# Decoder layer: expert rows taken out of group B's chains, and the query projection run on the unnormed residual

## The chip, the cores and the metric

The kernel runs on one core of one Trainium2 chip. The metric is the device time of one execution in microseconds (us). Before the change it is 4662.38 us, the median of three runs (4650.35 to 4666.11). The engines are TensorE (PE, with its weight load PEld), VectorE (DVE), ScalarE (ACT), GpSimd (POOL) and SyncE (SP); SP issues most transfers, POOL the indirect gathers.

## The reference, cut to what matters

One layer of a hybrid decoder, for 512 prompt tokens and 8 sample tokens, width 2048. A mixing block of three branches (gated linear attention, a spatial gating unit, cross-attention) is merged and multiplied by `w_out`. What follows is the part that the change is about:

```python
x  = x + merged @ w_out
h  = rmsnorm(x, norm_ffn_g)            # x * rsqrt(mean(x*x) + eps) * g
q  = (h @ w_q)                         # 2048 x 2048: 8 heads, 2 halves of 128
s1 = q[:, :, 0] . sub_k1;  s2 = q[:, :, 1] . sub_k2      # 128 keys each
# per head: the 16 best of each half, then the 16 best of their 256 sums:
# 8 x 16 = 128 experts of each token, with softmaxed gates
a    = peer_u[idx] . h                 # 128 gathered rows of 2048 per token
x    = x + sum(gate * gelu(a) * peer_v[idx])             # 128 more rows
y    = rmsnorm(x, norm_final_g)
```

The norm's divisor is one number per token, so that `(x * g) @ w_q * rstd` equals `h @ w_q`.

## The kernel before, in words

The tokens form two groups. Group A is 264 tokens (two units of 128, and the 8 samples), group B the other 256. Activations lie with their features on the partitions, in 16 tiles of 128. Each weight block is 128 x 2048 values of four bytes (1.05 MB) and gives one tile of 128 outputs. A gathered "row" below is an indirect transfer of one table row for each of 128 tokens: 1.05 MB too.

**Group A** runs first, in split precision: ACT writes a block's high part (`split_hi`, L559), DVE its low part (`split_lo`, L563), and TensorE takes three products per tile (L579). `split` has two slots, so block n + 1 is split while block n is multiplied. A's tail is `sp_out`, `act_out`, `dve_out` and `pe_out` (L2642 to L2801):

- 16 blocks of `w_out`. DVE adds each output to the residual x1, squares it and adds it to `ssum`.
- The norm: a column sum on PE (`pe_spread`), root on ACT, reciprocal on DVE, then 16 tiles h2 = x1 * g * rstd, split in pieces of four tiles. PE turns x1's three units meanwhile (L2758), and ACT copies them out to be stored.
- 16 blocks of `w_q` on h2; ACT copies each output to `pq`. DVE scales B's input `hxb2` once in between.
- After the last block: the key scores of unit 0 (L2765), h2 of unit 0 turned into `htok`, then h2 and the scores of the two other units, each through one of two `stage` buffers and out to DRAM. PE waits for the last of these copies (`staged`), then begins group B.
- DVE finds the experts of head 0 (`top_head`, L2896), and POOL's first gather follows.

**Group B** is multiplied in plain four-byte products (L640) from three `raw` buffers. Its stages are the projections (`dve_project_b`), the merge of branch A (N_BA), attention, the merge of branch C (N_BC), the spatial unit, the merge of branch B (N_BB), and `dve_out_b` with `w_out`, norm and `w_q`.

**A's experts** run beside group B. `experts_a` (L3114) is a generator on DVE: each step is one gathered row, 528 in all: 128 of `peer_u` (`dot`, L3107) and 128 of `peer_v` (`accumulate`, L3112) for each of units 0 and 1, then 16 for the samples. `beside(k)` in B's stages does k of these steps in DVE's program order; the number is written by hand at each place. Heads of later units are found between rows (`head_beside`, one each 14 rows of `peer_v` of unit 0). POOL gathers up to six rows ahead (`ring`), and only after A's last block, since `ring` lies over `split`. 295 rows are done in B's stages.

**The table** (`dve_table`, L3246) is 128 blocks of `peer_u`, multiplied with B's h2 (L3273). DVE's rows are spread evenly over its 128 places, up to row 509 (`U_ROWS`), together with B's 16 heads. ACT does the exponentials and gelus for both at fixed places: `act_gelu` at blocks 30 and 68, `act_soft` at 10, 44, 76 and 108 (L3221 to L3244). DVE's `soft_second` waits for them. Then `dve_last` and `pe_last` do B's experts, 256 more rows.

## Time and profile before

| what | us |
|---|---|
| median of three runs | 4662.38 (4650.35 to 4666.11) |
| the profiled execution | 4664.21 |
| its span in the profile | 4662.5 |
| PE, DVE, ACT, POOL busy | 4116.3, 3098.0, 916.1, 1309.7 |
| DMA over the span | 328 GB/s on average, 1528.97 MB |
| chain that ended last | PE 57%, DMA 22%, DVE 9% |

The span is the program's time between its first and last instruction; the execution's time is 1.7 us longer. In the tables by window, "DMA" is the share of time in which the core's 16 DMA engines were busy, "PEclk" the clock that TensorE was granted (1.00 is 2.4 GHz, 0.50 is 1.2 GHz), and "(x..)" counts instructions.

### The profile page before, as it was taken

What the parts mean: (1) busy time and instruction counts of PE and PEld (TensorE: products, weight loads), DVE (VectorE), ACT (ScalarE), POOL (GpSimd) and SP (SyncE); (2) the same over time, 40 slices, a digit from 0 to 9 for tenths busy, and PEclk for the clock granted to TensorE, in tenths of its full rate; (3) what the DMA queues carried; (4) which work ended last, traced back from release to release, by engine and by line L of the source; (5) the groups of instructions that cost most, each with busy time, mean ns of one, the idle gap of its engine ahead of it and who ended that gap; (6) DMA issues with size and microseconds to landing.
All of it is one profiled execution on the core that took longest, in us unless ns stands there. A gap on an engine that the chain in (4) does not pass through costs nothing.

```text
span 4662.5 us, 61529 instructions
## 1 busy us (share of the span) xinstructions
PE 4116.3 (88%) x23624; PEld 3587.9 (77%) x23624; DVE 3098.0 (66%) x4546; ACT 916.1 (20%) x1325; POOL 1309.7 (28%) x822
## 2 busy tenths in 40 slices
PE   7999999999899999999886788999999999577555
PEld 7999999999789887887775677887888888353222
DVE  7434344435557557887678786797788357688776
ACT  4334433324333321110000000000000004000100
POOL 0000000000000013444345233343345231467665
PEclk9999999999899999999998798999999999787777
DMA  5555678766356469999999799999899897999998
GB/s 215 197 205 190 220 282 294 274 242 206 124 206 234 164 265 410 414 393 404 423 388 404 314 405 408 393 423 414 354 414 423 357 364 277 412 406 399 422 421 356
DMA packets 303262, 1528.97 MB, mean 328 GB/s; under 512 B 36394, under 2 KB 108538, under 8 KB 134948
## 3 DMA queue, kind: packets, MB, share of 16 engines
q0 software_dynamic: 114288, 830.54, 43.3%
q1 hardware_dynamic: 188772, 695.78, 39.6%
q8 instruction: 122, 2.00, 0.2%
q14 instruction: 80, 0.66, 0.0%
HBM read 1450.06 MB, written 76.13 MB: 327 GB/s over the span
## 4 chain that ended last, share of the span: by engine, by line
PE 57%; DMA 22%; DVE 9%; issue 5%; DVEq 3%; POOL 3%; ACT 2%; ACTq 0%; SPq 0%; POOLq 0%
PE psum L579 27%; PE psum L3273 14%; DMA sb_ring<-in_peer_v,sb_idx_all 8%; PE psum L640 7%; DMA sb_raw<-in_wstream 4%; DMA sb_ring<-in_peer_u,sb_idx_all 3%; DMA sb_raw_u<-in_wstream 3%; POOL sb_ring L3086 2%; PE psum L3529 2%; DVE sb_ring L3107 1%; DVE sb_acc L3112 1%; PE psum L2325 1%; DVE sb_acc_b L3430 1%; PE psum L3511 1%; DVEq L2354 1%
## 5 line engine op out<-in xcount | busy, mean ns | idle before, releaser
L579 PE MATMUL psum<-sb_actr,sb_split 128*128 128x264 f32 x8112 | 1010.6, 286 | 36.5 <-DVE sb_split L563 20.4
L579 PEld LDWEIGHTS psum<-sb_actr,sb_split 128*128 128x128 f32 x8112 | 999.2, 190 | 42.4 <-issue 25.9
L563 DVE TENSOR_TENSOR sb_split<-sb_raw,sb_split 128x2048 fp32r<-128x2048 f32 x201 | 460.5, 2292 | 638.2 <-ACT sb_split L559 637.1
L2997 POOL DMA_INDIRECT sb_ring<-in_peer_u,sb_idx_all x256 | 413.2, 1614 | 1172.1 <-DVE sb_dots L3107 550.3
L3112 DVE SCALAR_TENSOR_TENSOR sb_acc<-sb_ring,sb_coef,sb_acc 128x2048 f32<-128x2048 f32 x256 | 601.7, 2350 | 130.7 <-DMA sb_ring<-in_peer_v,sb_idx_all 115.5
L3107 DVE CUSTOM_DVE_ANT_0 sb_ring<-sb_ring,sb_htok 128x2048 f32<-128x2048 f32 x264 | 594.8, 2290 | 128.7 <-DMA sb_ring<-in_peer_u,sb_idx_all 123.1
L2997 POOL DMA_INDIRECT sb_ring<-in_peer_v,sb_idx_all x256 | 433.3, 1693 | 667.8 <-DVE sb_acc L3112 575.3
L3529 PE MATMUL psum<-sb_ring,sb_diag 128*128 128x512 f32 x512 | 343.5, 833 | 244.4 <-DMA sb_ring<-in_peer_v,sb_idx_all 237.3
L3430 DVE SCALAR_TENSOR_TENSOR sb_acc_b<-sb_ring,sb_coef_b,sb_acc_b 128x2048 f32<-128x2048 f32 x192 | 451.3, 2351 | 133.2 <-DMA sb_ring<-in_peer_v,sb_idx_all 119.5
L3086 POOL DMA_INDIRECT sb_ring<-in_peer_v,sb_idx_all x256 | 431.3, 1685 | 270.7 <-DVE sb_acc_b L3430 130.3
L3529 PEld LDWEIGHTS psum<-sb_ring,sb_diag 128*128 128x128 f32 x512 | 132.3, 272 | 440.2 <-DMA sb_ring<-in_peer_v,sb_idx_all 270.6
L3273 PE MATMUL psum<-sb_h2b,sb_raw_u 128*128 128x256 f32 x2048 | 453.0, 381 | 12.0 <-DMA sb_raw_u<-in_wstream 10.1
L3273 PE MATMUL psum<-sb_h2b,sb_raw 128*128 128x256 f32 x2048 | 451.3, 380 | 9.8 <-DMA sb_raw<-in_wstream 9.7
L3273 PEld LDWEIGHTS psum<-sb_h2b,sb_raw_u 128*128 128x128 f32 x2048 | 388.5, 191 | 72.9 <-DMA sb_raw_u<-in_wstream 18.4
L3273 PEld LDWEIGHTS psum<-sb_h2b,sb_raw 128*128 128x128 f32 x2048 | 387.3, 190 | 70.1 <-DMA sb_raw<-in_wstream 18.2
L559 ACT ACTIVATE sb_split<-sb_raw 128x2048 fp32r<-128x2048 f32 x201 | 384.4, 1913 | 203.1 <-PE psum L579 168.1
L640 PE MATMUL psum<-sb_hxb,sb_raw 128*128 128x256 f32 x1824 | 406.3, 385 | 8.3 <-DMA sb_raw<-in_wstream 6.3
L640 PEld LDWEIGHTS psum<-sb_hxb,sb_raw 128*128 128x128 f32 x1824 | 350.3, 193 | 60.7 <-DMA sb_raw<-in_wstream 8.6
L579 PE MATMUL psum<-sb_actb_hi,sb_split 128*128 128x256 f32 x1664 | 299.8, 279 | 0.0
L579 PEld LDWEIGHTS psum<-sb_actb_hi,sb_split 128*128 128x128 f32 x1664 | 257.0, 188 | 0.0
L579 PE MATMUL psum<-sb_actb_lo,sb_split 128*128 128x256 f32 x832 | 232.2, 279 | 0.0
L3229 ACT ACTIVATE sb_a_tile<-psum 128x128 f32<-128x128 f32 x128 | 35.5, 278 | 852.2 <-PE psum L3273 852.2
(446 smaller groups left out, 4216.7 us busy)
## 6 DMA issues: line engine op xcount, KB each, us to landing
sb_raw<-in_wstream SPq DMA_DIRECT2D x398, 1024.0 KB, 7.8
sb_raw_u<-in_wstream SPq DMA_DIRECT2D x64, 1024.0 KB, 16.3
sb_states<-in_state SPq DMA_DIRECT2D x32, 512.0 KB, 3.9
sb_states_t<-in_stateT SPq DMA_DIRECT2D x32, 512.0 KB, 4.4
out_gla_s<-sb_states SPq DMA_DIRECT2D x32, 512.0 KB, 3.1
dram_z<-sb_zst SPq DMA_DIRECT2D x121, 132.0 KB
dram_z_b<-sb_zst SPq DMA_DIRECT2D x65, 128.0 KB
sb_vrow<-dram_v SPq DMA_DIRECT2D x8, 1024.0 KB, 5.4
```

What stands on the lines that cost most here:

```text
L559: nc.scalar.activation(split[:, slot, 0, :], raw[:, slot, :], ACT.Copy).then_inc(hi_ready, 1)
L563: nc.vector.tensor_tensor(split[:, slot, 1, :], raw[:, slot, :], split[:, slot, 0, :], ALU.subtract).then_inc(lo_ready, 1)
L579: last = nc.tensor.matmul(psum[:, bank, 0:ntok], w[a], acts(b, kt), start=(i == 0 and a == 0 and b == 0), stop=(i == len(kts) - 1 and a == 1))
L640: last = nc.tensor.matmul(bank_b(q), raw[:, k % 3, w0 + i * P:w0 + (i + 1) * P], acts[:, kt, 0:WB], start=(i == 0), stop=(i == len(kts) - 1))
L2325: last = nc.tensor.matmul(psum[:, 6 + j % 2, 0:WB], raw[:, k % 3, kt * P:(kt + 1) * P], hxb2[:, kt, :], start=(kt == 0), stop=(kt == KT - 1))
L2997: nc.gpsimd.indirect_dma_start(ring[g % RING][:], None, ins[table], bass.IndirectOffsetOnAxis(ap=col, axis=0)) \
L3086: nc.gpsimd.indirect_dma_start(ring_b[slot_b(y, n)][:], None, ins["peer_v"], bass.IndirectOffsetOnAxis(ap=idx_all[:, 3 + y, n:n + 1], axis ...
L3107: nc.vector.tensor_tensor_reduce(u[:], u[:], htok[:], 1.0, 0.0, ALU.mult, ALU.add, out).then_inc(row_used, 1)
L3112: nc.vector.scalar_tensor_tensor(out=a[:], in0=v[:], scalar=c, in1=a[:], op0=ALU.mult, op1=ALU.add).then_inc(row_used, 1)
L3273: last = nc.tensor.matmul(bank_b(OUTS_U + i), raw_u[u_slot(i)][:, kt * P:(kt + 1) * P], h2b[:, kt, :], start=(kt == 0), stop=(kt == KT - 1))
L3430: nc.vector.scalar_tensor_tensor(out=acc_b[y][:], in0=v[:], scalar=coef_b[y][:, n:n + 1], in1=acc_b[y][:], op0=ALU.mult, op1=ALU.add).then ...
L3529: last = nc.tensor.matmul(psum[:, b, :], diag[:, n // PE_EACH % DIAGS, :], v[:, b * 512:(b + 1) * 512], start=(n < PE_EACH), stop=(n >= SL ...
```

## The change

In A's tail the products of `w_q` start on x1 * g, tile by tile as `w_out`'s outputs come, without waiting for the norm; `rstd` is multiplied in where DVE now evicts `pq`. Blocks are split two ahead. The turnings of x1 and h2, and the scores of the first four heads, are put between the `w_q` blocks on PE. Two heads of unit 0 are routed on DVE, in halves, during blocks 11 to 14; later ones are found two heads ahead of their rows. `h2` now lies in x1's place, and `stage0` alone takes x1's three units.

In B's stages 33 `beside` steps go away: 6 in the first merge, 6 in attention, 8 in the merge of branch C, 8 in the spatial unit, 5 in the norm. The total is fixed, so these rows are done in the table.

```diff
+        h2 = x1
+        gx1_hi = sb("gx1_hi", [P, KT, WA], F32R, R_M + 16896)
+        gx1_lo = [sb("gx1_lo0", [P, 7, WA], F32R, R_RAW + 16384), ...
@@ load_b: B's third raw buffer
+                if k == 2:
+                    sp.wait_ge(out_ready, OUTS_A)
@@ dve_attention
-                    beside(2)
                     maxima(h + 2)
-                    beside(1)
                     divide(h + 2)
@@ dve_spatial
                 norm_gv_first(dve, g, u)
-                beside(3)
                 norm_gv_second(dve, g, u)
                 if u > 0:
-                    beside(1)
                     gate_gv(dve, g, u - 1)
-            beside(1)
             gate_gv(dve, g, g.units - 1)
@@ stage_of
-            return k % 2 if k < STAGED_A else (k - STAGED_A) % 2
+            return 0 if k < 3 else k % 2 if k < STAGED_A else (k - STAGED_A) % 2
@@ act_out
+            for j in range(KT):
+                split_next(act, N_OUT + j)
+                act.wait_ge(evac_done, out_of(N_OUT + j) + 1)
+                nc.scalar.activation(gx1(0, j), x1[:, j, :], ACT.Copy, scale=pcols[:, C_FFN + j:C_FFN + j + 1])
+                if j > 0:
+                    act.wait_ge(act_lo, 20 + j)
+                nc.scalar.activation(sq2[:], x1[:, j, :], ACT.Square).then_inc(act_hi, 1)
@@ dve_out
+            for j in range(KT):
+                n = N_OUT + j
+                dve.wait_ge(out_ready, out_of(n) + 1)
+                nc.vector.tensor_tensor(x1[:, j, :], pair_of(n % 2), x1[:, j, :], ALU.add).then_inc(evac_done, 1)
+                split_lo(dve, n + 2, n % 2)
+                dve.wait_ge(act_hi, 20 + j + 1)
+                nc.vector.tensor_tensor(ssum[:], ssum[:], sq2[:], ALU.add)
+                nc.vector.scalar_tensor_tensor(out=gx1(1, j), in0=x1[:, j, :], scalar=pcols[:, C_FFN + j:C_FFN + j + 1],
+                                               in1=gx1(0, j), op0=ALU.mult, op1=ALU.subtract).then_inc(act_lo, 1)
+            for c in range(16):
...
+                nc.vector.tensor_tensor(pq[:, c, :], pair_of(n % 2), rstd[:], ALU.mult).then_inc(evac_done, 1)
+                if n + 2 < N_END:
+                    split_lo(dve, n + 2, n % 2)
+                if 2 <= c < 6:            # hxb2, four tiles in each
...
+                if c in (6, 7):           # h2, eight tiles in each
...
+                if HEAD_AT <= c < HEAD_AT + 2 * HEADS_AHEAD:
+                    half_head_ahead(dve, *divmod(c - HEAD_AT, 2))
@@ pe_out: after block c of w_q; X1_AT, H2_AT, SCORE_AT, HEAD_AT = (2, 4, 6), 8, 10, 11
+                if c == H2_AT:
+                    pe.wait_ge(staged, 3)
+                    pe.wait_ge(normed, 10)
+                    turn_unit(h2, 0, 4).then_inc(turned, 1)
+                if c == SCORE_AT:
+                    pe.wait_ge(htok_ready, 1)
+                    score_unit(0, 4, range(8)).then_inc(scored, 1)
+            pe.wait_ge(evac_done, OUTS_A)
+            score_unit(0, 4, range(8, KT)).then_inc(scored, 1)
@@ dve_out_b
-            beside(6)
+            beside(1)
@@ experts_a
-            top_head(dve, 0, 0)
-            dve.drain().then_inc(idx_ready, 1)
...
+                    if t == 0 and n % TOP == 0 and n // TOP + HEADS_AHEAD < PH:
@@ vector's program
-            dve_merge_b(dve, N_BA, N_BC, beside, lambda k: 3 if k < GATES_B else 2)
+            dve_merge_b(dve, N_BA, N_BC, beside, lambda k: 3 if k < GATES_B and k % 2 == 0 else 2)
-            dve_merge_b(dve, N_BC, N_BB, beside, lambda k: 2 - k % 2)
+            dve_merge_b(dve, N_BC, N_BB, beside, lambda k: 1)
```

## Rows read from the trace of the kernel before

**Rows 1.** Windows: start:end, length, busy of each engine, PEclk, DMA share, GB/s.

```profile
1683.00:1703.00 20.00, 17.34 (x147) 15.46 (x148) 12.01 (x57) 11.10 (x7) 3.01 (x3) 1.00 0.39 148
1703.00:2222.00 519.00, 487.44 (x2367) 418.82 (x2365) 409.73 (x591) 69.99 (x137) 208.44 (x130) 0.97 0.99 405
2222.00:2426.00 204.00, 183.79 (x832) 160.56 (x832) 142.93 (x178) 11.65 (x20) 83.42 (x49) 0.95 0.99 410
2426.00:2462.00 36.00, 23.85 (x81) 18.74 (x82) 29.45 (x49) 8.67 (x25) 19.45 (x10) 0.74 0.94 361
2462.00:2551.00 89.00, 59.82 (x256) 50.41 (x255) 76.38 (x104) 1.03 (x1) 44.80 (x22) 0.86 1.01 410
2551.00:2596.00 45.00, 19.81 (x56) 12.38 (x56) 39.48 (x65) 2.09 (x4) 13.78 (x10) 0.50 0.74 277
2596.00:2669.00 73.00, 60.40 (x256) 51.44 (x256) 56.80 (x84) 0.43 (x1) 18.08 (x15) 0.92 0.84 336
2669.00:2823.00 154.00, 121.48 (x546) 105.78 (x546) 123.76 (x155) 4.17 (x3) 54.95 (x42) 0.87 1.00 409
```

**Rows 2.** Windows of the table, the whole and three parts; columns as in group 1.

```profile
2952.00:3870.00 918.00, 897.46 (x4098) 776.03 (x4098) 679.53 (x1161) 65.57 (x270) 370.07 (x222) 1.00 0.96 392
3242.00:3300.00 58.00, 57.20 (x264) 49.73 (x263) 15.93 (x42) 5.16 (x18) 9.32 (x6) 1.00 0.73 281
3300.00:3682.00 382.00, 373.75 (x1710) 322.97 (x1710) 322.50 (x518) 27.53 (x114) 177.68 (x98) 1.00 1.01 418
3682.00:3760.00 78.00, 77.50 (x358) 67.60 (x357) 19.60 (x11) 5.10 (x23) 14.90 (x9) 1.00 0.69 261
```

**Rows 3.** Timeline of PE in A's tail: start, us, what, [idle before <-releaser].

```profile
1569.00 0.71 PE L1238 MATMUL psum<-sb_ssum,sb_ones 128*128 128x264 f32 x2 [1.71 <-DVEq L2730]
1570.23 7.13 PE L2758 MATMUL psum<-sb_ident,sb_x 128*128 128x128 f32 x48 [0.53 <-DVE sb_ssum L2732]
...
1683.26 3.81 PE L2765 MATMUL psum<-sb_keys,sb_pq 128*128 128x128 f32 x32 [0.61 <-ACTq L2698]
...
1702.36 27.89 PE L640 MATMUL psum<-sb_hxb,sb_raw 128*128 128x256 f32 x128 [1.96 <-ACT sb_stage L2635]
```

**Rows 4.** Groups by line, 1605 to 1683: count, busy us, mean ns.

```profile
L579 PE MATMUL psum<-sb_actr,sb_split 128*128 128x264 f32 x624 | 77.1, 287 | 2.9 <-DVE sb_split L563 2.9
...
L563 DVE TENSOR_TENSOR sb_split<-sb_raw,sb_split 128x2048 fp32r<-128x2048 f32 x13 | 29.7, 2292 | 43.2 <-ACT sb_split L559 42.9 <-issue 0.3
L559 ACT ACTIVATE sb_split<-sb_raw 128x2048 fp32r<-128x2048 f32 x12 | 22.9, 1910 | 0.1
```

**Rows 5.** Timeline of DVE: one head, its first operation, its middle, its last.

```profile
1689.09 0.49 DVE L2904 MAX8 sb_top_v<-sb_sc 128x8 f32<-128x128 f32 x2 [13.38 <-ACT sb_sc L2700]
...
1692.45 0.18 DVE L2920 CAST sb_top_if<-sb_top_i 128x32 f32<-128x32 uint32 x1
...
1698.15 0.18 DVE L2946 SCALAR_TENSOR_TENSOR sb_idx_all<-sb_e_f 128x16 uint32<-128x16 f32 x1
```

**Rows 6.** Chain of waits, 1690 to 1740: a small store once gathers run.

```profile
1709.98 13.36 DMA dram_z_b<-sb_zst
```

**Rows 7.** Groups of DVE by line, 1703 to 2952: expert rows.

```profile
L3112 DVE SCALAR_TENSOR_TENSOR sb_acc<-sb_ring,sb_coef,sb_acc 128x2048 f32<-128x2048 f32 x128 | 300.7, 2349 | 44.6 <-DMA sb_ring<-in_peer_v,sb_idx_all 38.1 <-DVE sb_acc L3112 1.4 <-issue 0.3
```

**Rows 8.** Timeline of PE in B's stages: where it waited for DVE.

```profile
2426.36 6.14 PE L2063 MATMUL psum<-sb_kvt,sb_xq 128*128 128x256 f32 x16 [9.37 <-DVE sb_merged L2352]
...
2551.47 3.68 PE L2409 MATMUL psum<-sb_ident,sb_gv_b 128*128 128x128 f32 x16 [13.21 <-DVE sb_zst L2352]
...
2586.00 2.07 PE L2420 MATMUL psum<-sb_bspat,sb_ones 1*128 1x512 f32 x2 [12.58 <-DVE sb_vn L2518]
...
2823.49 84.98 PE L640 MATMUL psum<-sb_h2b,sb_raw 128*128 128x256 f32 x384 [15.55 <-DVEq L2859]
```

**Rows 9.** Timeline of DVE in the table: its two long waits for ACT.

```profile
3283.77 0.29 DVE L2965 TENSOR_REDUCE sb_sums<-sb_gate_all 128x8 f32<-128x128 f32 x1 [41.15 <-ACT sb_gate_all L2975]
...
3738.95 0.29 DVE L2965 TENSOR_REDUCE sb_sums<-sb_gate_all 128x8 f32<-128x128 f32 x1 [63.11 <-ACT sb_gate_all L2975]
```

More of the change, by code:

```diff
@@ L593, in of_b, with gx1 @@
             return actb[b][:, kt, :]
+        def gx1(b, kt):
+            return gx1_lo[kt // 7][:, kt % 7, :] if b else gx1_hi[:, kt, :]
         def of_br2(b, kt):
@@ L2560, in dve_spatial_beside, with dve_spatial @@
                 gated_lo(dve, 2)
-        def dve_spatial(dve, g, beside):
+        def dve_spatial(dve, g):
             dve.wait_ge(vn_stored, 16)
@@ L2650, in sp_out @@
             wide_loop(sp, N_OUT + 4, N_WQ, lambda n, slot, u, m, j: load_block(sp, n + 3, 1 - slot))
-            for u in range(3):
-                store_stage(sp, u, x1_dram[x1_rows(GA, u), :], unit(u)[0])
-            wide_loop(sp, N_WQ, N_END - 4, lambda n, slot, u, m, j: load_block(sp, n + 3, 1 - slot))
-            load_block(sp, N_END - 1, (N_END - 1) % 2)
+            for n in range(N_WQ, N_END - 3):
+                load_block(sp, n + 3, (n + 3) % 2)
+                if n - N_WQ in (4, 6, 8):
+                    u = (n - N_WQ - 4) // 2
+                    store_stage(sp, u, x1_dram[x1_rows(GA, u), :], unit(u)[0])
             for k in range(3):
@@ L2665, in act_out @@
             act_piece(act, merged, 3)
-            wide_loop(act, N_OUT, N_WQ, lambda n, slot, u, m, j: split_hi(act, n + 1, 1 - slot, u + 1 + slot, m))
-            act.wait_ge(sums_ready, 6)
-            act.wait_ge(root_in, ROOTS_X1[0] + 1)
-            nc.scalar.activation(rstd[:], ssum[:], ACT.Sqrt).then_inc(root_out, 1)
-            def x1_stage(u):
-                rows = unit(u)[0]
-                act.wait_ge(turned, u + 1)
-                fill_stage(act, u, rows, psum[0:rows, 4 - 4 * (u % 2):8 - 4 * (u % 2), :])
@@ new lines, in act_out @@
+            for j in range(KT):
[6 more added lines that the diff above has]
+            for c in range(16):
+                split_next(act, N_WQ + c)
+                if c == 0:
+                    act.wait_ge(root_in, ROOTS_X1[0] + 1)
+                    nc.scalar.activation(rstd[:], ssum[:], ACT.Sqrt).then_inc(root_out, 1)
+                if c in X1_AT:
+                    u = X1_AT.index(c)
+                    rows = unit(u)[0]
+                    act.wait_ge(turned, u + 1)
+                    fill_stage(act, u, rows, psum[0:rows, 4:8, :])
+                if c == H2_AT:
+                    act.wait_ge(turned, 4)
+                    nc.scalar.activation(htok[:].rearrange("p (b f) -> p b f", b=4), psum[:, 4:8, :], ACT.Copy).then_inc(htok_ready, 1)
+                if c == SCORE_AT:
+                    act_scores(act, 0)
@@ L2709, in act_out, with act_scores @@
                 rows = unit(1 + k)[0]
-                act.wait_ge(scored, 2 + k)
+                act.wait_ge(scored, 3 + k)
                 fill_stage(act, 5 + k, rows, psum[0:rows, 4 * (k % 2):4 * (k % 2) + 4, :])
+        def act_scores(act, half):
+            act.wait_ge(scored, half + 1)
+            nc.scalar.activation(sc[0][:, 4 * half:4 * half + 4].rearrange("p h a k -> p (h a k)").rearrange("p (b f) -> p b f", b=2),
+                                 psum[:, 4 + 2 * half:6 + 2 * half, :], ACT.Copy).then_inc(sc_ready_b, 1)
         def dve_out(dve):
@@ L2733, in dve_out @@
-            dve.wait_ge(root_out, ROOTS_X1[0] + 1)
-            nc.vector.reciprocal(rstd[:], rstd[:])
-            dve.drain()
-            for q in range(4):
-                for kt in range(4 * q, 4 * q + 4):
-                    nc.vector.scalar_tensor_tensor(out=h2[:, kt, :], in0=x1[:, kt, :], scalar=pcols[:, C_FFN + kt:C_FFN + kt + 1],
-                                                   in1=rstd[:], op0=ALU.mult, op1=ALU.mult)
-                dve.drain().then_inc(normed, 1)
-                if q > 0:
-                    dve_piece(dve, h2, 20, q - 1)
@@ L2759, in turn_unit, with score_unit @@
             return last
-        def score_unit(u, b0):
+        def score_unit(u, b0, tiles=range(KT)):
             rows, tok = unit(u)
-            for c in range(KT):
+            for c in tiles:
                 last = nc.tensor.matmul(psum[0:rows, b0 + c // 4, (c % 4) * P:(c % 4 + 1) * P],
@@ L2773, in body @@
                 pe.wait_ge(evac_done, m - 1)
-                products(pe, slot, of_a, range(KT), 0, 2 * slot, WA, ready=ready).then_inc(out_ready, 1)
+                products(pe, slot, acts, range(KT), 0, 2 * slot, WA, ready=ready).then_inc(out_ready, 1)
             body(N_OUT, N_OUT % 2, None, N_OUT + 16, 0, ready=lambda kt: wait_piece(pe, kt, 16))
@@ L2948, in top_head, with half_head_ahead @@
             dve.drain()
+        def half_head_ahead(dve, k, half):
+            if half == 0:
+                dve.wait_ge(pool_made, 1)
+                dve.wait_ge(sc_ready_b, 1)
+                top_first(dve, 0, k)
+            else:
+                top_second(dve, 0, k)
+                dve.drain().then_inc(idx_ready, 1)
         def heads_of(x, t):
@@ L3644, in _ @@
             dve_out_b(dve, beside)
-            assert 270 < gone[0] < 300, gone
+            assert 250 < gone[0] < 300, gone
             dve_table(dve, beside, gone[0])
```

175 lines of the change are left out of this document (84 added, 91 removed).

## The prediction

> **What bounds the kernel now.** I read the windows first, stage by stage, because the engines' shares of the whole span hide that the limit changes. From the first gather on it is the DMA engines: they are busy 0.99 to 1.01 of B's projections, first merge, merge of branch C and output stage, and of most of the table [rows 1, 2], at 405 to 418 GB/s. What follows the table is not edited, and I let it stand. So the reader should count two things: bytes, which the change leaves alone, and time in which the DMA engines idle. That idle time, (1 - share) times length, is 12 us in 1683 to 1703, 5 + 2 + 2 in the next three windows, 12 in the spatial unit, 12 in the merge of branch B [rows 1], and 16 + 24 in the table's two holes [rows 2] (by its whole share of 0.96 it would be 37): 85 us in all.
>
> The second view is PE's timeline. In B's stages it stands still for DVE, not for data: 9.37 us before attention, 13.21 before the spatial unit, 12.58 inside it, 15.55 before `w_q` [rows 8]. DVE was late because rows stood ahead of B's work in its program: one is 2.35 us [rows 7], one head 9.2 us (1689.09 to 1698.33) [rows 5]. The third view is DVE's timeline in the table, where it is the other way round: DVE waits 41.15 and 63.11 us for ACT's exponentials, which stand at fixed blocks [rows 9]. Rows have room there, in B's chains they have none.
>
> **Price of a moved row.** 1.05 MB at the 418 GB/s of 3300 to 3682 [rows 2] is 2.5 us of DMA, more than its 2.35 us of DVE. 33 rows are 83 us of DMA wherever they go.
>
> **Part 1, A's tail.** One `w_q` block is 48 products, 77.1 / 624 x 48 = 5.9 us [rows 4]. PE's last `w_out` product ends at 1569.00 - 1.71 = 1567.3, its last `w_q` product at 1683.26 - 0.61 = 1682.6 [rows 3]. These 115.3 us hold 16 x 5.9 = 94.4 us of blocks, and 0.7 and 5.7 of column sum and x1's turnings (7.13 less waits): 14.5 us idle, round the norm. The change lets `w_q` begin at once, so this goes. Added to this stretch: h2's turning (16 where x1 has 48, so 1.9) and half of unit 0's scores, 3.81 / 2 = 1.9 [rows 3]. New waits, from DVE's order. Per block DVE needs 1.91 (ACT's high part) + 2.29 + 0.45 for the eviction [rows 4]: 4.7 of 5.9 us. (a) `rstd` between blocks 0 and 1: about 1 us late. (b) h2 is scaled in 16 operations over blocks 6 and 7 and PE waits for the last: 2 us. (c) A head's second half is 5.9 us (1692.45 to 1698.33), its first 3.4 [rows 5]. The second halves at blocks 12 and 14 do not fit into 5.9 - 4.7: the first delays block 15 by 1.8 us, the second delays the last eviction, and with it the scores, by 4.4. Extra copies on ACT (0.4 us each) fit beside its 1.9 of 5.9 us. So the last block ends 14.5 - 3.8 - 1 - 2 - 1.8 = 5.9 us earlier, near 1677, and gathers may start then instead of behind head 0, at 1698.33 or later.
>
> But what follows is not earlier by as much. B's first product waits for the last staged copy (the 1.96 us) [rows 3], and that copy waits in `stage1` for the store of h2's unit 1. Before, that store went out ahead of the gathers. Now it goes out some 10 us after six gathers of 1.05 MB were issued. The nearest row is the small store that took 13.36 us once gathers ran [rows 6]; the other bound is one transfer's own 2.5 us. I take 13: the second scores wait 4.4 us for the eviction and take 1.9, a turning 1.9, a copy 1.9 (10 in all), the store 13, two copies 1.9 each: 1677 + 27 = 1704, a little less where they overlap, against 1702.36. B's start: **0** (bounds -7 and +5).
>
> The Trainium skill, page "DMA: Bandwidth & Descriptors", section "Queues, rings and completion order", says that each DMA engine takes turns between its queues, packet by packet. Beside one gather queue the store would then have half of the rate, 5 us instead of 13, and B would begin near 1695; the row of 13.36 us speaks against counting on it.
>
> **Part 2, B's projections.** The 131 rows stay. DVE has two heads (18 us) behind it, and six rows are in the ring 20 us earlier. Of PE's 32 us of waits there (519 - 487) [rows 1] part is for DVE. But the share is 0.99: what can be won is the earlier 15 us of DMA work, and PE must use it. I take **-8** (0 to -18).
>
> **Part 3, the chains.** First merge: 6 rows are 14 us of DVE, which clears the 9.37 us wait [rows 8]; of the 11 us in which PE waits for weights, 4 more: **-13** (-6 to -20). Attention, 36 us with PE busy 24 at a clock of 0.74: DVE's answers no longer sit behind one or two rows: **-7** (-4 to -9). Merge of branch C: 89 us at share 1.01, PE busy 60 at clock 0.86; 8 rows are 20 us of DMA, and a head (9.2) goes with them; the 13.21 us DVE wait vanishes and most weight waits: **-25** (-14 to -32), down to about PE's 60. Spatial: 8 rows and one head, 8 x 2.35 + 9.2 = 28 us of DVE, PE 20 us at the low clock 0.50; the waits of 10 and 12.58 go, its own chain of norms stays: **-18** (-12 to -22). Merge of branch B: **-2**. Output stage: five rows in front of the norm are -13, but the heads shift with the row count and one more falls into its 32 rows, +6 of its 9.2: **-7** (0 to -13). Sum of part 3: **-72**. The clock needs no term of its own: it is in the durations of those windows.
>
> **Part 4, the table.** It gets 247 rows instead of 214. Before it took 918 us (2952 to 3870) with 40 of DMA idle: 878 busy. Plus 83 is 961; with DVE's two long waits gone the idle time falls to near nothing. PE is busy for 897 [rows 2], so the DMA decides: 960, **+42**. Lower bound +15: the rows fill the two holes and the rest is paid by DMA time that weight loads do not need at the end. Upper +60, if rows starve the weight loads as well. ACT's block 30 needs the 64th dot of unit 1, row 320, which stands at place 30 of DVE's program (it was 15): at 1.93 x 2.35 + 9.2/4 = 6.8 us of DVE per place against 7.2 of PE it is just in time.
>
> **Sum.** 0 - 8 - 72 + 42 = **-38** against the profiled 4664.2: 4626. The median of the runs is 1.8 us lower, so 4662.4 - 38 = **4624 us**. The check: 85 us of idle DMA, less 38 gained, plus 6 from the earlier end of A, leaves 53 us idle, which the now row-free spatial and attention stages (some 15 and 10), projections and ends can hold.
>
> **Rivals.**
> (1) *The DMA keeps its sum.* Every stage but two had a share near 1; taking rows out of B's chains makes DMA idle there exactly as much as it fills up in the table. For it: the spatial unit already idles with rows beside it (0.74) and the ring holds only six. Against: the waits of rows 8 are on DVE, and the chain of waits goes through them. Then only the earlier gathers count: -8 to -12, 4652. The Trainium skill, page "Perfetto Trace Analysis", section "Identifying the Most-Contended Engine", says that interleaving regimes with different limits may help; this change undoes such an interleaving.
> (2) *Slower: the table pays full price and starves.* With both waits gone DMA is saturated through all 128 blocks, each weight load stands behind six gathers, and ACT stands at block 30 until DVE reaches row 320. It decides if DVE needs over 7.2 us per place in the first 30. The table then takes +83 and 15 for stalls, B's chains give -60 and B's start +5, projections -8: +35, about 4697.
> (3) *The table absorbs nearly all.* +10 there, with parts 2 and 3 at their better ends (-15, -72): 4585.
> (4) The rows move, but A's tail, where DVE now evicts, splits, scales and routes, is late by more than computed. It costs at most 10 us and moves no sign; it is in the range. That the change does not do what it says I see no way for: the counts are in program order.
>
> **How the numbers follow.** Forecast 0.58, (1) 0.16, (2) 0.08, (3) 0.18. Spreads of the terms added by size give 4624 +- 22; reaching to (3) and to (1) the range is **4585 to 4657**. A measurement of this kernel can tell some 0.3% (14 us) from nothing: faster means below 4648. From the forecast 0.55, from (3) 0.18, from (1) 0.04: **faster 0.77**; same 0.03 + 0.12 = **0.15**; slower **0.08**.
>
> **What would show it.** Part 1: `w_q`'s first product within 1 us of `w_out`'s last; gaps of some 2 us before block 15 and 4 before the second scores; a first gather near 1678; B's first product near 1702, waiting for a staged copy that waits for a store. Part 3: the four waits of rows 8 below 3 us, B's stages to the table 80 us shorter, with a DMA share under 0.6 in the spatial unit. Part 4: the table near 960 us, share above 0.98, DVE's waits for ACT under 10 us. Wrong is the forecast if the table grows by over 60 us or under 15, or if the chains give under 50.

## The result, and the profile after

The changed kernel takes **4640.62 us** (median of 8 runs, 4634.76 to 4648.66), the kernel before, beside it on the same chip, 4663.74 us (8 runs, 4650.35 to 4668.09). The ratio is 0.9948, with a 95% interval of 0.9937 to 0.9960: 0.5% faster, by 23 us where 38 were forecast. The profiled execution took 4642.09 us with a span of 4640.0, against 4662.5 before.

Read the windows first, as for the kernel before. Their columns are those of [rows 1].

```profile
2222.00:2418.00 196.00, 184.27 (x832) 160.91 (x832) 121.05 (x136) 12.71 (x20) 74.22 (x44) 0.97 0.96 391
2418.00:2454.00 36.00, 19.84 (x87) 16.32 (x88) 19.75 (x55) 9.60 (x25) 2.03 (x3) 0.81 0.60 235
2454.00:2530.00 76.00, 58.67 (x260) 50.68 (x259) 55.83 (x84) 0.00 (x0) 14.69 (x15) 0.87 0.97 395
2530.00:2555.00 25.00, 19.40 (x53) 11.93 (x52) 13.03 (x17) 2.52 (x4) 0.07 (x1) 0.57 0.20 79
...
2890.00:3846.00 956.00, 909.42 (x4098) 770.66 (x4098) 754.68 (x1228) 65.23 (x268) 401.75 (x256) 1.00 1.01 417
```

The spatial unit (2530) is 25 us long instead of 45 and leaves the DMA engines idle for 0.80 of it. The table (last line) is 956 instead of 918 us, at a share of 1.01 where it was 0.96: its 40 us of idle DMA are gone.

The timeline of PE, where it waits in A's tail and in B's stages, answers to [rows 3] and [rows 8]:

```profile
1565.25 0.28 PE L582 MATMUL psum<-sb_gx_hi,sb_split 128*128 128x264 f32 x1
...
1629.97 3.65 PE L2778 MATMUL psum<-sb_ident,sb_x 128*128 128x128 f32 x16 [5.52 <-DVEq L2770]
...
1672.53 0.36 PE L582 MATMUL psum<-sb_gx_hi,sb_split 128*128 128x264 f32 x1 [2.10 <-DVE sb_split L566]
...
1682.61 3.78 PE L2785 MATMUL psum<-sb_keys,sb_pq 128*128 128x128 f32 x16 [4.01 <-DVE sb_pq L2753]
...
1705.23 5.00 PE L648 MATMUL psum<-sb_hxb,sb_raw 128*128 128x256 f32 x14 [6.72 <-ACT sb_stage L2642]
...
1864.65 3.07 PE L1782 MATMUL psum<-sb_qi_b,sb_ki_b 128*32 128x32 f32 x32 [13.77 <-DVEq L1939]
...
2418.34 3.72 PE L2071 MATMUL psum<-sb_kvt,sb_xq 128*128 128x256 f32 x16 [0.52 <-DVE sb_merged L2358]
2435.56 1.11 PE L2108 MATMUL psum<-sb_ident,sb_prob 128*128 128x128 f32 x4 [13.49 <-DVE sb_prob L2180]
...
2502.24 16.64 PE L648 MATMUL psum<-sb_brb,sb_raw 128*128 128x256 f32 x64 [8.02 <-DMA sb_raw<-in_wstream]
2528.19 3.48 PE L2415 MATMUL psum<-sb_ident,sb_gv_b 128*128 128x128 f32 x16 [9.31 <-DVE sb_zst L2358]
2534.87 2.04 PE L2426 MATMUL psum<-sb_bspat,sb_ones 1*128 1x512 f32 x2 [3.20 <-DVE sb_vn L2524]
...
2761.25 4.21 PE L648 MATMUL psum<-sb_h2b,sb_raw 128*128 128x256 f32 x9 [2.34 <-DVEq L2887]
```

Of the four waits of [rows 8] (9.37, 13.21, 12.58, 15.55 us) three are at 0.52, 3.20 and 2.34; the one before the spatial unit is still 9.31. New ones stand beside them: 13.49 us inside attention, 13.77 at the first chunk product of the projections (5.08 before), 8.02 for a weight block.

**One correction before stages are compared.** Executions differ ahead of anything that was edited: `w_out`'s last product in A ends at 1567.3 before and at 1565.3 after, and in the twelve experiments between 1557.3 and 1567.6. So all that follows is in lengths, from that product to the table's last block, and not in times of the clock:

| stage, us | before | after | change | forecast |
|---|---|---|---|---|
| A's tail, to B's first product | 135.1 | 140.0 | +4.8 | 0 |
| projections | 529.2 | 530.7 | +1.5 | -8 |
| first merge | 194.8 | 182.4 | -12.4 | -13 |
| attention | 35.4 | 34.2 | -1.2 | -7 |
| merge of branch C | 89.7 | 75.7 | -14.0 | -25 |
| spatial unit | 45.0 | 25.2 | -19.8 | -18 |
| merge of branch B | 72.8 | 72.5 | -0.3 | -2 |
| output stage, to `w_q` | 154.2 | 135.4 | -18.8 | -7 |
| `w_q` of B | 128.7 | 129.0 | +0.3 | |
| table | 917.9 | 956.3 | +38.4 | +42 |
| sum | 2302.8 | 2281.4 | -21.4 | -38 (rounded) |

The sum, the 2.0 us by which this execution was early and 1.0 us more after the table make the 22.5 us between the spans.

Each length is read from one execution, and lengths repeat unequally where the code of a stage is the same. A's tail comes out at 140.0 to 140.3 us in the six kernels that have the changed one and at 135.1 to 136.3 in the three with the old one. The projections take 529.2 to 534.0 us in the three with the old tail and 524.1 to 533.0 in five with the new one. From the table's last product to the end of the program, which nothing edits, it is 788.4 to 798.3 us. So 2 us tell something in the tail, and 5 us in the projections or in a sum can be the execution's own.

What the table pays is seen in two waits views of it, first of the kernel before, then after (columns: engine, line, releaser; us in total, times, the longest):

```profile
DVE sb_sums L2965 <- ACT sb_gate_all L2975: 104.8, 3, 63.1
...
PE psum L3273 <- DMA sb_raw_u<-in_wstream: 10.1, 21, 1.4
PE psum L3273 <- DMA sb_raw<-in_wstream: 9.7, 20, 1.4
```

```profile
PE psum L3318 <- DMA sb_raw_u<-in_wstream: 23.8, 46, 1.4
PE psum L3318 <- DMA sb_raw<-in_wstream: 22.4, 46, 1.4
...
DVE sb_sums L3011 <- ACT sb_gate_all L3021: 16.2, 1, 16.2
```

DVE's long waits for ACT shrank from 104.8 to 16.2 us, and PE's waits for weights grew from 19.8 to 46.2. With PE's busy time up from 897.5 [rows 2] to 909.4 this is the whole of the 38.4 us (26.4 + 12.0). In the chain of waits of the changed kernel the table is now this pattern, over and over, where the chain before had 3% of the span in that transfer and now has 11%:

```profile
3289.46 23.01 DMA sb_raw_u<-in_wstream
...
3312.51 7.19 PE psum L3318 x32
...
3319.72 24.01 DMA sb_raw_u<-in_wstream
```

### The profile page after: what moved, and what is told of

It reads as the page before. It is cut to its first block, busy times and chain, and to the rows that moved or that the text cites. A ratio compares the mean times of both kernels' runs of the same rounds, so it can differ in the third digit from the quotient of the medians.

```text
span 4640.0 us, 61274 instructions
## 1 busy us (share of the span) xinstructions
PE 4125.0 (89%) x23624; PEld 3579.6 (77%) x23624; DVE 3099.4 (67%) x4558; ACT 918.0 (20%) x1338; POOL 1288.8 (28%) x822
## 4 chain that ended last, share of the span: by engine, by line
PE 55%; DMA 26%; DVE 8%; issue 4%; POOL 2%; DVEq 2%; ACT 2%; SPq 0%; ACTq 0%; POOLq 0%
PE psum L582 28%; DMA sb_raw_u<-in_wstream 11%; PE psum L648 9%; PE psum L3318 9%; DMA sb_ring<-in_peer_v,sb_idx_all 7%; DMA sb_ring<-in_peer_u,sb_idx_all 3%; POOL sb_ring L3132 2%; DMA sb_raw<-in_wstream 2%; PE psum L3574 2%; PE psum L2331 1%; DVE sb_acc L3158 1%; DVE sb_ring L3153 1%; PE psum L3556 1%; DVE sb_acc_b L3475 1%; DVE sb_split L566 1%
## 5 line engine op out<-in xcount | busy, mean ns | idle before, releaser
L582 PE MATMUL psum<-sb_actr,sb_split 128*128 128x264 f32 x7344 | 913.3, 286 | 29.5 <-DVE sb_split L566 18.4
L582 PEld LDWEIGHTS psum<-sb_actr,sb_split 128*128 128x128 f32 x7344 | 903.1, 190 | 33.9 <-issue 18.9
L3043 POOL DMA_INDIRECT sb_ring<-in_peer_u,sb_idx_all x256 | 428.8, 1675 | 1118.8 <-PE psum L582 519.8
L3043 POOL DMA_INDIRECT sb_ring<-in_peer_v,sb_idx_all x256 | 392.4, 1533 | 719.0 <-DVE sb_acc L3158 632.0
L3132 POOL DMA_INDIRECT sb_ring<-in_peer_v,sb_idx_all x256 | 435.7, 1702 | 267.7 <-DVE sb_acc_b L3475 144.2
```

Of the source, the lines that this page charges most:

```text
L582: last = nc.tensor.matmul(psum[:, bank, 0:ntok], w[a], acts(b, kt), start=(i == 0 and a == 0 and b == 0), stop=(i == len(kts) - 1 and a == 1))
L3043: nc.gpsimd.indirect_dma_start(ring[g % RING][:], None, ins[table], bass.IndirectOffsetOnAxis(ap=col, axis=0)) \
L3132: nc.gpsimd.indirect_dma_start(ring_b[slot_b(y, n)][:], None, ins["peer_v"], bass.IndirectOffsetOnAxis(ap=idx_all[:, 3 + y, n:n + 1], axis ...
```

## The experiments

Twelve kernels. "Before" stands beside each on the same chip; the median is in us, the ratio is to the kernel before. "Tail", "chains" (B's first product to the table's first), "table" and their "sum" are lengths in the profiled execution; "rows" is how many rows more than before the table does.

| kernel | rows | tail | chains | table | sum | median (runs) | ratio (95%) |
|---|---|---|---|---|---|---|---|
| before | 0 | 135.1 | 1249.8 | 917.9 | 2302.8 | 4663.7 | |
| tail_only | 0 | 140.2 | 1253.2 | 914.4 | 2307.8 | 4663.88 (10) | 1.0010 (1.0000 to 1.0019) |
| spatial_only | 8 | 136.3 | 1226.6 | 915.5 | 2278.4 | 4635.84 (5) | 0.9953 (0.9940 to 0.9967) |
| fifteen | 15 | 134.6 | 1209.3 | 923.5 | 2267.4 | 4626.45 (5) | 0.9921 (0.9908 to 0.9934) |
| rows_back | 19 | 140.1 | 1206.6 | 927.9 | 2274.5 | 4632.82 (6) | 0.9946 (0.9927 to 0.9964) |
| twenty | 20 | 136.3 | 1196.9 | 931.1 | 2264.3 | 4623.36 (6) | 0.9918 (0.9905 to 0.9931) |
| four_edits | 26 | 136.4 | 1182.8 | 945.2 | 2264.4 | 4621.52 (5) | 0.9919 (0.9906 to 0.9933) |
| rows_only | 33 | 136.2 | 1192.0 | 957.5 | 2285.7 | 4644.77 (8) | 0.9960 (0.9949 to 0.9972) |
| after | 33 | 140.0 | 1185.1 | 956.3 | 2281.4 | 4640.62 (8) | 0.9948 (0.9937 to 0.9960) |
| early_rows | 33 | 140.1 | 1175.2 | 956.8 | 2272.0 | 4634.24 (4) | 0.9944 (0.9927 to 0.9961) |
| stores_early | 33 | 135.2 | 1183.8 | 957.1 | 2276.0 | 4636.84 (5) | 0.9947 (0.9929 to 0.9964) |
| att_head | 34 | 140.3 | 1173.5 | 961.6 | 2275.3 | 4638.02 (5) | 0.9959 (0.9945 to 0.9973) |
| all_three | 34 | 136.2 | 1166.4 | 963.5 | 2266.2 | 4626.44 (6) | 0.9921 (0.9905 to 0.9938) |
| more_out | 41 | 140.1 | 1182.3 | 967.5 | 2289.8 | 4644.66 (8) | 0.9963 (0.9950 to 0.9976) |

### The two halves of the change

**tail_only**: A's tail as changed, all of B's `beside` numbers as before (in attention, the spatial unit and the output stage too).

```diff
-            dve_merge_b(dve, N_BA, N_BC, beside, lambda k: 3 if k < GATES_B and k % 2 == 0 else 2)
+            dve_merge_b(dve, N_BA, N_BC, beside, lambda k: 3 if k < GATES_B else 2)
...
-            dve_merge_b(dve, N_BC, N_BB, beside, lambda k: 1)
+            dve_merge_b(dve, N_BC, N_BB, beside, lambda k: 2 - k % 2)
...
```

> Group A's tail as changed, but B's stages with all the rows they had before (295, none moved to the table). Theory (the rows carry the gain, the tail almost none): A's last block ends 4 us earlier, but B's first product still waits for a staged copy behind a store of h2, so B begins at 1705 +- 3 and its first merge at 2227 +- 5; the table begins at 2950 to 2958; total within 8 us of the kernel before, 4656 to 4672. Rival (the tail and the 20 us earlier gathers carry it): the first merge begins by 2212, total 4650 or less.

**rows_only**: the kernel before, with the 33 rows taken out.

> Group A's tail as before, the 33 rows moved from B's stages to the table. Theory (DVE's lateness in the chains was the price, DMA in the table pays for part of it): first merge begins at 2223 as before, table at 2887 to 2893, table 38 us longer (918 to 956); total -24 to -32 against before, 4632 to 4640. Rival (rows only change places while the DMA engines are the bound): table begins earlier by no more than it grows, total within 8 us of before.

The new tail alone is worth nothing: 1.0010, and its length is 5 us more than before, not less. The rows alone bring 15 us in the median and 17.1 in the sum of lengths, below what was expected of them. So the gain comes from the rows, and the query projection's early start, the larger part of the diff, gives none by itself. Whether it adds a little once the rows are out is not shown: the changed kernel is at 0.9948 and rows_only at 0.9960, with intervals that overlap, and their sums are 4.3 us apart.

### What the tail loses

**stores_early**: SP issues the stores of x1's three units one block earlier (the blocks at which PE turns them and ACT copies them into `stage0` stay).

```diff
-                if n - N_WQ in (4, 6, 8):
-                    u = (n - N_WQ - 4) // 2
+                if n - N_WQ in (3, 5, 7):
+                    u = (n - N_WQ - 3) // 2
```

> The changed kernel with the three stores of x1's units issued one query-projection block earlier each, behind blocks 3, 5 and 7 instead of 4, 6 and 8. Now ACT waits 5.8 and 7.5 us for them, writes block 8's high part late, and PE waits 5.5 us before h2's turning. Theory: that wait falls to 2 us (h2's scaling by DVE alone), A's last block ends 3 to 5 us earlier, near 1674; B's first product follows it by 26 us as before, near 1701; B's projections still end at 2232 +- 5, since DVE and the rows set that, so the total is within 4 us of the changed kernel's 4641. Rival (time won in A's tail is won in the total): -4 us or more.

The changed kernel's timeline of ACT shows why h2's turning was 5.52 us late, not the 2 that the forecast gave it:

```profile
1605.46 1.88 ACT L2642 ACTIVATE sb_stage<-psum 128x2048 f32<-128x2048 f32 x1 [5.78 <-DMA dram_x<-sb_stage]
...
1620.57 1.87 ACT L2642 ACTIVATE sb_stage<-psum 8x2048 f32<-8x2048 f32 x1 [7.50 <-DMA dram_x<-sb_stage]
```

All three units go through `stage0`, each copy waits for the store of the one before, and ACT's split of the next block stands behind it in its program. With the stores a block earlier the copies of the second and the third unit have no wait, and PE's is 1.92 (timelines of ACT and PE of stores_early):

```profile
1611.82 1.86 ACT L2642 ACTIVATE sb_stage<-psum 8x2048 f32<-8x2048 f32 x1
```

```profile
1625.22 2.91 PE L2778 MATMUL psum<-sb_ident,sb_x 128*128 128x128 f32 x16 [1.92 <-DVEq L2770]
...
1677.67 3.45 PE L2785 MATMUL psum<-sb_keys,sb_pq 128*128 128x128 f32 x16 [4.02 <-DVE sb_pq L2753]
```

The last block now ends 109.6 us after `w_out` (1677.67 - 4.02 - 1564.08), where the forecast's own figures give 1677 - 1567.3 = 109.7; in the changed kernel it is 113.3. The tail is 135.2 us, as before the change. The 5 us are in the trace; the medians can't tell them (0.9947 against 0.9948).

That even this tail wins nothing is the other end of it, which the forecast had: the chain of waits of the changed kernel before B's first product.

```profile
1689.14 1.89 ACT sb_stage L2642
...
1691.05 10.42 DMA dram_h<-sb_stage
...
1703.33 1.86 ACT sb_stage L2642
...
1705.23 29.61 PE psum L648 x128
```

h2's store took 10.42 us among the gathers that had started earlier. By the Trainium skill's rule of turns between queues ("DMA: Bandwidth & Descriptors", "Queues, rings and completion order") the estimate was 5; the trace does not bear out a half share for the store.

### What the projections lose

**early_rows**: the same 131 rows in B's projections, but more of them early.

```diff
-            beside(7)
+            beside(13)
...
-            beside(3)
+            beside(6)
...
-            beside(26)
+            beside(17)
```

> The changed kernel with nine rows of B's projections earlier: 13 instead of 7 before the decay's first step, 6 instead of 3 before its second, 17 instead of 26 in front of the first products; the count at the end of the stage is the same. DVE now idles 45 of 60 us there with the ring full, and PE later waits 13.8 us for it. Theory: that wait falls to under 3 us, the first merge begins 8 to 13 us earlier (2214 to 2219), total 4628 to 4634. Rival (rows are held by their landing, not by where they stand): the wait falls but weight loads come late by as much, first merge within 3 us of 2227, total 4638 to 4643.

Windows at the start of the projections, of the changed kernel and of early_rows:

```profile
1703.00:1723.00 20.00, 17.77 (x74) 15.40 (x75) 2.63 (x4) 3.01 (x5) 4.08 (x3) 0.86 1.01 425
1723.00:1743.00 20.00, 20.00 (x84) 16.71 (x83) 6.75 (x11) 0.89 (x4) 0.24 (x1) 0.91 0.80 300
1743.00:1763.00 20.00, 20.00 (x94) 17.61 (x93) 4.04 (x5) 9.10 (x12) 4.81 (x3) 1.00 0.87 354
1763.00:1783.00 20.00, 20.00 (x95) 17.60 (x94) 19.43 (x25) 1.92 (x9) 5.67 (x3) 1.00 0.68 247
```

```profile
1727.00:1747.00 20.00, 18.94 (x79) 15.78 (x79) 10.20 (x15) 0.89 (x4) 4.62 (x3) 0.91 1.01 412
1747.00:1767.00 20.00, 18.76 (x85) 15.55 (x84) 18.21 (x47) 8.98 (x12) 8.38 (x6) 1.00 1.02 427
1767.00:1787.00 20.00, 12.96 (x47) 10.61 (x46) 19.07 (x25) 1.15 (x5) 6.76 (x4) 0.74 1.01 416
```

In the changed kernel DVE, two heads ahead, has done its first rows by 1706 and then stands before the decay step, with 2.63, 6.75 and 4.04 us of work in 20. The view of its waits from 1700 to 1765, POOL's with them:

```profile
POOL sb_ring L3043 <- DVE sb_dots L3153: 35.1, 1, 35.1
DVE sb_bcum L1999 <- PE psum L1790: 30.3, 1, 30.3
DVE sb_bcum L2007 <- ACT sb_gy L1870: 16.0, 1, 16.0
```

The ring is full, POOL sends no gather for 35.1 us, and the DMA share falls to 0.80, 0.87, 0.68: (0.20 + 0.13 + 0.32) x 20 = 13 us of idle DMA, about what the earlier gathers had won. It is missed later: in the chain of waits ahead of the first chunk product (the wait of 13.77 us) stand a gather of 19.27 us, a head and rows:

```profile
1826.23 19.27 DMA sb_ring<-in_peer_u,sb_idx_all
```

With six more rows early the share is 1.01 and that wait is gone; the projections take 516.7 us instead of 530.7, the first merge gives 4.6 of it back (187.0), and the sum of lengths is 9.4 lower. The two stages together take 703.3 to 706.8 us in the three kernels with these rows early and 711.0 to 716.0 in the five that are otherwise alike in them, so this is more than one execution's luck. The two ratios do not tell it (0.9944 and 0.9948).

### What attention loses

**att_head**: the one `beside(1)` that the change left in attention goes too.

```diff
             maxima(1)
-            beside(1)
             divide(0)
```

> The changed kernel less the one row that is left in B's attention (it goes to the table). That row is the one that carries a head: 9.3 us of head and 2.4 of row stand between the maxima and the division, and PE waits 13.5 us. Theory: the head falls behind attention into the merge of branch C, where PE is four outputs ahead; attention 34 to 24 us, total -6 to -10 against the changed kernel, 4630 to 4635. Rival (the DMA engines are the bound there, so that the time only moves): attention shorter, the merge of branch C or the table longer by as much, total within 3 us.

The changed kernel's timeline of DVE in attention:

```profile
2422.95 0.48 DVE L2934 MAX8 sb_top_v<-sb_sc 128x8 f32<-128x128 f32 x2
...
2432.31 2.35 DVE L3158 SCALAR_TENSOR_TENSOR sb_acc<-sb_ring,sb_coef,sb_acc 128x2048 f32<-128x2048 f32 x1
2434.58 0.16 DVE L2178 RECIPROCAL sb_small<-sb_small 128x2 f32<-128x2 f32 x1
```

That single step is a row at which a head falls due, so it costs 9.2 + 2.35 us between `maxima(1)` and `divide(0)`: the 13.49 us of PE's wait. Without it the wait is 1.86 us and attention 20.8 us:

```profile
2420.29 0.66 PE L2108 MATMUL psum<-sb_ident,sb_prob 128*128 128x128 f32 x4 [1.86 <-DVE sb_prob L2180]
```

Of these 13.4 us the merge of branch C takes 4 back (the head is found there) and the table is 5 longer, with a 34th row in it. In the medians nothing is left of it (0.9959 against 0.9948), so that the -6 to -10 expected for the total are not borne out.

### What a row costs in the table

**rows_back**: of the changed kernel's 33 rows, the 8 of the spatial unit and the 6 of attention go back. **more_out**: 8 more rows leave the merge of branch B. **spatial_only**: the kernel before, with only the spatial unit's 8 out.

```diff
@@ rows_back, in dve_attention and dve_spatial
+                    beside(2)
...
+                    beside(1)
...
+                beside(3)
...
+                    beside(1)
...
+            beside(1)
@@ more_out
-            dve_merge_b(dve, N_BB, N_OUT, beside, lambda k: 1)
+            dve_merge_b(dve, N_BB, N_OUT, beside, lambda k: k % 2)
@@ spatial_only, in dve_spatial
-                beside(3)
...
-                    beside(1)
...
-            beside(1)
```

> The changed kernel with 14 rows put back from the table: 8 in the spatial unit, 6 in attention. Theory (a row in the now saturated table costs a whole 2.5 us of DMA, in the spatial unit 2.35 us of DVE plus a head of 9.3): spatial unit 25 to 45 us, attention 34 to 36 or less if the head falls elsewhere, the table 956 to 921 to 926; total -5 to -12 against the changed kernel, 4629 to 4636. Rival (rows beside a chain are the worst place, as the change has it): total +10 or more, the table shorter by 15 at most, since DVE again waits for ACT's fixed places in it.

> The changed kernel with 8 more rows out of the merge of branch B (one at every second output), so 255 in the table. Theory (the table is saturated, each row costs it 2.5 us; in the merge, PE busy 59 of 72 us, they cost little): table 956 to 976, merge of branch B 72 to 64, total +10 to +14, 4651 to 4655. Rival (the table still has room for rows): total within 3 us or below.

> The kernel before with only the spatial unit's 8 rows taken out (they are done in the table). The forecast put -18 on this part, and the changed kernel shows the stage 20 us shorter. Theory A (the rows only change their place: the DMA pays for them in the table, at the 2.0 us a row that the kernel with 14 rows put back showed, 28.4 us of table for 14 rows): spatial unit 45 to 25, merge of branch B and the rest unchanged, table +8 to +16 longer, total -4 to -10 and perhaps nothing that can be told. Theory B (the spatial unit's idle DMA time is won for good, since the table of before has 40 us of idle DMA of its own to take the rows): table +4 at most, total -15 to -18, about 4645.

Spatial_only is the surprise of the study: **eight rows alone give 24 us, as much as the whole change** (0.9953 against 0.9948). The unit is 20 us shorter, the merge of branch B 7.7 (65.1), and the table does the eight rows in 2.4 us less than before (in 1.1 more than in tail_only, the other kernel with none). Of the theories on record the one that had these rows paid for in the table fell; the other (-15 to -18 us) was right in kind, and too low for a reason that it did not name. The window and the waits of its table:

```profile
2920.00:3836.00 916.00, 896.67 (x4101) 774.92 (x4102) 698.14 (x1177) 65.49 (x270) 387.90 (x230) 1.00 0.98 402
```

```profile
DVE sb_sums L2962 <- ACT sb_gate_all L2972: 78.0, 3, 45.2
...
PE psum L3270 <- DMA sb_raw_u<-in_wstream: 10.7, 22, 1.4
PE psum L3270 <- DMA sb_raw<-in_wstream: 7.9, 21, 0.4
```

The 7.7 us of the merge of branch B do not look like the rows' own. The number of rows done before a stage also sets where in it the next head falls. The merge takes 64.8 and 65.1 us in the two kernels in which its head stands behind the fourth or fifth of its 16 rows (four_edits and spatial_only), and 71.1 to 73.0 in the eleven in which it stands behind the eleventh or twelfth. Timeline of DVE, in spatial_only 21 us into the stage (it begins at 2572.4), in the kernel before 48 us into it (2596.5):

```profile
2593.48 0.48 DVE L2901 MAX8 sb_top_v<-sb_sc 128x8 f32<-128x128 f32 x2
```

```profile
2644.13 0.48 DVE L2904 MAX8 sb_top_v<-sb_sc 128x8 f32<-128x128 f32 x2
```

Waits of DVE in that stage, of spatial_only and of the kernel before:

```profile
DVE sb_zst L2352 <- PE psum L640: 6.2, 5, 5.3
```

```profile
DVE sb_zst L2352 <- DMA sb_gt<-dram_z_b: 4.0, 1, 4.0
DVE sb_zst L2352 <- DMA sb_gt_b<-dram_z_b: 3.2, 2, 2.1
```

With a late head DVE first waits for the loads of the gates, 5.9 to 7.4 us in all eleven, and then finds the head on top of it. With an early one it is behind from then on and waits for them 0.0 and 0.4 us. No run moved the head alone, but the traces leave some 17 of the 24 us to the rows. The spatial unit's own 20 us hold a head too: four_edits has the eight rows there and no head, and takes 36.2 us, so that the rows are worth 11 and the head 9.

The rows went into DVE's waits for ACT and the DMA idle time beside them (share 0.96 to 0.98), and PE's waits for weights stayed at 18.6 us (19.8 before). Read down the table of runs: with 0, 8, 15, 19, 20, 26, 33, 34 and 41 rows the table is 914 to 918, 916, 924, 928, 931, 945, 956 to 958, 962 to 964 and 968 us. The first eight are free, the next eleven or so cost 1 us each, and from 20 rows to 34 it is (962.6 - 931.1) / 14 = 2.2 us each, near the 2.5 us of DMA that a row needs. The last point does not go on like that: from 33 rows to 41 it is 11.2 us, 1.4 each, and from 20 to 41 1.7 on average. So the price rises once the idle time is filled, but over no longer stretch does a row pay the whole 2.5. Rows_back shows the other side: the last 14 rows shortened the chains by 21.5 us (1206.6 - 1185.1) and lengthened the table by 28.4. Some 20 of the 21.5 are the spatial unit's (45.2 there); the 7.9 us that attention gains by its six rows the merge of branch C gives back (67.9 us in rows_back, 75.7 after). These 6.9 us of sum are not told by the ratios (0.9946 against 0.9948). More_out: eight rows out of the merge of branch B bring 12.9 us there (59.6), the output stage gives 7.9 back, the table pays 11, where 20 were expected of it.

### Versions made from it

**all_three** is att_head, early_rows and stores_early together; **four_edits** is that with the spatial unit's 8 rows back; **fifteen** is all_three with the rows of the first merge, of the merge of branch C and of the norm back, so that only attention (7) and the spatial unit (8) are free of rows; **twenty** is fifteen without the norm's five.

> The changed kernel with all three edits: no row in B's attention, nine rows earlier in B's projections, x1's stores one block earlier. Theory: attention's -8 and the projections' -7 lie in different stages and add; the stores add nothing: table to begin near 2868, select near 3832, total 4624 to 4629. Rival (what is won before the table is lost in it): 4632 to 4637, no better than either alone.

> The kernel with three edits (no row in attention, rows later in B's projections, x1's stores one block earlier; 4626.4, 0.9921) and the spatial unit's 8 rows put back. If the rows of the spatial unit are free or better there, as the kernel with 14 rows put back suggested (33 rows moved gave 4640.6, 19 rows moved 4632.8): spatial unit 45 us instead of 25, table about 940 instead of 963, total 4615 to 4625. Rival: the gain of putting rows back belonged to the table's ends or to attention's rows, and with the other three edits the last 8 are worth nothing or cost: 4627 to 4640.

> The kernel with three edits, and of its 34 rows out of B's chains only the 15 of attention (7) and the spatial unit (8) stay out; the first merge, the merge of branch C and the norm of the output stage have theirs back. Theory C (a row's price in the table is marginal: nothing for about the first 16, which fill its idle 40 us of DMA, and 2 to 2.5 us for each after that; read from 8 rows -2 us, 19 rows +10, 33 rows +38, 41 rows +50): table 918 to 926. Attention 21 us, spatial unit 25, merge of branch B 65 to 69; the first merge and the merge of branch C near 190 and 85 to 90; from B's first product to the end of the table 2120 to 2128 (2130 with 34 rows), total 4616 to 4624. Rival D (every row costs 1.2 us there, as 38 us for 33 suggests): table 936, total 4628 to 4636.

> The same with 20 rows out: also the five ahead of the output stage's norm. Theory C: the output stage 10 to 15 us shorter than with 15 rows, the table 928 to 934, so within 6 us of the kernel with 15 rows, 4614 to 4624, since rows past the 16th pay 2 to 2.5 us each. Rival D: table 942, 4622 to 4632. Neither asks for more than 5 us below the kernel with three edits (4626).

All four beat both kernels, by 0.8% against before: 4621.52 to 4626.45 us, with intervals that overlap. The spatial unit's eight rows put back (four_edits) change nothing that can be told, 0.9919 against 0.9921 for all_three. In fifteen and twenty the table came out as the marginal price says (923.5 and 931.1; the rival of 1.2 us a row asked for 936 and 942), but the chains of fifteen were longer than expected, so that B's first product to the end of the table was 2132.8 us and not 2120 to 2128, and the median of 4626.45 lies above the 4616 to 4624 on record. Its merge of branch C holds 22 rows and two heads, 22 x 2.35 + 2 x 9.2 = 70 us of DVE where PE needs 60, and in the kernel before 23 rows and one head; it takes 94.2 us (89.7 before), and the spatial unit waits (timeline of PE in fifteen):

```profile
2529.33 3.04 PE L2414 MATMUL psum<-sb_ident,sb_gv_b 128*128 128x128 f32 x13 [22.80 <-DVE sb_zst L2357]
```

With 15, 20, 26 and 34 rows out, the sum of lengths of these four stays within 2264 to 2268 us. There each row out of a chain wins about what the table asks for it, and how many are out hardly matters any more. Some 7 us of four_edits are those of the early head in the merge of branch B.

## Why the prediction was right or wrong

**Right:** the direction, the range (4585 to 4657) and the main mechanism: PE stood behind rows in DVE's program, and the table took these rows in for less than their full DMA price. Part 3 as a sum: -72 forecast, -66.2 measured (the rows of the table above from the first merge to the output stage, less 0.3 in `w_q`). Part 4: the DMA's account, 878 us busy and 83 more, gave 960 (+42) and it is 956 (+38.4), at share 1.01. The stages after the table did not move by more than 1 us. That part 3's sum is so near is partly luck: attention and the merge of branch C gave 16.8 us less than forecast, the output stage 11.8 more. Of the signs that the forecast named, B's stages to the table are 65 us shorter where 80 stood, and DVE still waits 16.2 us for ACT where under 10 stood.

**Part 1, B's start at 0: +4.8.** The step that failed is (b), "PE waits for the last of them: 2 us". It was 5.52, since x1's three stores went through one buffer and I had counted ACT's copies as fitting "beside its 1.9 of 5.9 us" without the stores that each waits for. stores_early shows it: 1.92 us, the last block at 109.6 of the 109.7 forecast, the tail 135.2. The rest of the part held: no gap at `w_q`'s start (1565.25, with `w_out`'s last product ending at 1565.4), 2.10 and 4.01 us where 1.8 and 4.4 stood, the first gather at 1679.6 where 1678 stood, a store of 10.42 where I took 13. The 0 itself was rounded down: the forecast's own sum gave 1704 against 1702.36.

**Part 2, -8: +1.5.** The premise "PE must use it" failed: nothing used the early DMA time, since DVE came to its fixed place before the decay step with the ring full and idled. It was in the text that the 131 rows stay, but not where in the program they stand. early_rows shows that this is the cause (-9.4). The +1.5 itself is one pair of executions: over the three kernels with the old tail and five with the new one the projections take 532.3 and 529.2 us on average, so that the part may be worth -3.

**Part 3, single terms.** Attention, -7: -1.2. The forecast says nothing of the one step that remained and did not count at which row the heads fall due; att_head shows 13.4 us for it. The merge of branch C, -25: -14.0; of its waits 8.02 us for a weight and 9.31 for DVE stayed, where the forecast had the DVE wait vanish and most of the others. The output stage, -7: -18.8. The +6 for one more head was wrong: two heads fall into the stage, but among the rows beside `w_out`, where nothing waits for them, and ahead of the norm there is none; and 6.0 us that DVE had waited for gathers there are gone too. The others are within 2 us.

Added up, the terms missed by 4.8 + 9.5 + 5.8 - 3.6 = 16.5 us, which is the gap between 38 and 21.4. In this pair of executions more than half of it is part 2.

**The rivals.** (1), that the DMA keeps its sum, was the wrong account for the first rows and near the right one for the last: spatial_only wins 24 us on 8 rows, some 17 of them by the rows themselves, rows_back shows 14 rows that won 21.5 us and cost 28.4. The sentence of the Trainium skill ("Perfetto Trace Analysis", "Optimization Strategy", the heading after the one that the prediction names) that interleaving regimes may help is borne out only from there on. (2), slower: the table took +38, not +83, and DVE's waits for ACT fell to 16 us. (3), that the table absorbs nearly all: so it was with eight rows, not with 33. (4), A's tail late, came true at half of its bound.

**Not settled:** why the table pays 1.4 us a row from 33 to 41 rows after 2.2 before that; what the head's place alone is worth in the merge of branch B; whether the new tail adds anything beside the rows; and a tail in which h2's store goes out ahead of the gathers, which was not tried.

## What to carry to other kernels

Price moved work at the margin, in the stage that takes it in: the first units fill its idle time and are free (eight rows here), later ones cost up to most of their share of the resource that is then full (2.2 of 2.5 us), so move the steps that win most in their chain and stop where the two prices meet. Where helper steps are placed by hand, look at what each placed step holds (here one in fourteen held a 9.2 us head) and at where the costly one lands when the count before it changes, or the place of a head is taken for the worth of the rows. And let the ring of transfers never stand full in front of a long wait. A long chain of work that is started earlier wins nothing if its last link, here one store, then runs against traffic that was started earlier too.

## What the runs showed of the hardware that was not expected

A weight block of 1.05 MB takes 23 to 24 us from its issue to its landing in the saturated table, though PE's single waits for it are 1.4 us at most: what shows in the waits view as many small waits is in the chain of waits a transfer of 23 us after every 7.19 us of products. A saturated stage is told by the share (1.01, at 417 GB/s), not by the length of its waits. And executions of the same code differ by up to 9 us before group B begins (`w_out` ending between 1558.4 and 1567.6 in kernels that are alike up to there) while the changed tail behind it repeats within 0.3 us (140.0 to 140.3 in six kernels): there the lengths between two marks of one execution tell 5 us apart, where medians of 5 to 8 runs could not. It is so of the tail alone: the projections of the same code vary by up to 9 us (524.1 to 533.0), and what follows the table by 10 (788.4 to 798.3).
